# Earlier turns for a background program: VectorE runs its state-space steps in six more turns while the first input tiles are multiplied

## The chip, the core and the metric

One core of one Trainium2 chip runs the program. The metric is the device time of one execution in microseconds (us). Every time below is from the one profiled execution unless a median is named.

## The reference, cut to what matters

Two blocks run one after the other on a sequence of about 1,000 tokens of width 1024, each with a token mixer and a feed-forward part. The change lies in the first block's token mixer, in which a state-space model (S5) works on `u`, the first 512 columns of the input projection:

```python
h = rmsnorm(x, g_pre)
proj = h @ w_in
u, q, k, v, o, gi, gf, ga, gb = jnp.split(proj, IN_SPLITS, axis=-1)
y_a = jax.nn.gelu(s5_ssm(u, lam_re, lam_im, b_re, b_im, c_re, c_im, d, log_dt))
...
# in s5_ssm
ab_re = mag * jnp.cos(lam_im * dt)
ab_im = mag * jnp.sin(lam_im * dt)
...
bu_re = jnp.einsum('blgh,gph->blgp', u, bb_re)
_, _, x_re, x_im = lax.associative_scan(_complex_affine_combine, (a_re, a_im, bu_re, bu_im), axis=1)
```

The kernel does the scan over blocks of eight tokens. For that it needs, before any `u` is used, tables that depend on the weights alone: powers of the complex number `ab` for 130 block positions (`E`), its first eight powers times `bb` (the operand `Bop`), and times `c` (the operand `Cop`).

## The kernel before

**Weights and tiles.** Each weight tile (128 x 1024) goes through three steps before TensorE can use it. The SyncE queue loads it into one of two buffers `w_raw` (`load_weight`, L278), ScalarE rounds it into one of three `w_hi` (`split_act`, L287, an operation recorded at L163), and VectorE subtracts to get one of three `w_lo` (`split_dve`, L296, recorded at L166). TensorE multiplies each slice three times, w_hi by X_hi, w_hi by X_lo and w_lo by X_hi, and waits for both parts of a tile before the tile's first matmul. The load of tile i waits until both parts of tile i-2 are made; the rounding of tile i waits until TensorE is done with tile i-3, whose buffer it takes. `next_tile(L, K, ahead)` at tile i makes the part of tile i+2 (for the loads, i+4).

**The stage around the change.** After the norm of the input (`prenorm_*`), TensorE takes tiles 0 to 2 (`u0` to `u2`) together, in nine groups of matmuls: three column chunks of 264, 264 and 512 (`c` = 0, 1, 2), and in each chunk the three tiles `t` (`FIRST`, `first_pe`, L920). Then come single tiles, three chunks each: tile 3 (`u3`), tiles 4 to 7 (`v0` to `v3`), and so on (`in1_pe`, L967). `first_act` and `in1_act` move the results out on ScalarE. `first_dve` and `in1_dve` hold VectorE's share, which here is only the low parts of the weights; VectorE waits for no result of these tiles.

**The background program.** The state-space work is written as one generator for each engine (`ssm_pe`, `ssm_act`, `ssm_dve`), cut in steps by `yield`. It is laid between the instructions of the foreground when the program is built: `tick()` puts in the next `rate` steps (3 in this stage), and `pause(n)` is n steps without an instruction. On an engine the order is then fixed, and instructions run in that order; across engines only semaphores order them. In `first_dve` a tick stands ahead of each low part, and the low part of tile 3 is made after the tick of `c` = 2, `t` = 0.

When this stage begins, 9 steps of `ssm_dve` are used up (one at the start, 8 in the norm). Step 10 makes `bb` and `Bn`, step 11 the eighth power, steps 12 to 23 the table `E` (12 steps: lengths 1, 2, 4, 8 and 16 in one each, 32 in two, 64 in four, the last 2 in one), and steps 24 to 30 the seven `powers(0)` written to `ssm_W`. Then come a pause, the four steps of `outputs(0)`, another pause, and the scans.

**What hangs on it.** ScalarE has `inputs(0)` at the last tick of tile `v0` (it waits for `powers(0)` and writes `ssm_Bop`) and `outputs(0)` at the last tick of `v1` (it waits for VectorE's `outputs(0)` and writes `ssm_Cop`). VectorE's `outputs(0)` begins in the last tick of `v0` and waits for `ssm_Bop`. TensorE's first state-space matmuls (group `k`, 0, recorded at L126) stand after `v1` and wait for `ssm_Cop`. Eight dummy matmuls, and some elsewhere (`WARM`), keep TensorE running ahead of chosen groups; the groups of `u3` and of (`k`, 0) have none.

Of the kernel before, what the change touches and what calls it, by code (L numbers as in the profile page):

```python
# [303 lines left out]
def next_tile(L, K, ahead):  # L304

    i = L.tile
    L.tile += 1
    if i and ahead is not None:
        ahead(L, K, i + (4 if ahead is load_weight else 2))
    return i  # L310
# [140 lines left out]
def pause(n):  # L451
    for _ in range(n):
        yield
# [274 lines left out]
def ssm_dve(V, K):  # L728
# [60 lines left out]
    def powers(j):  # L789

        a64r, a64i = ar2[:, 64 * j:64 * j + 64], ai2[:, 64 * j:64 * j + 64]
        pw = s.pw
        V.after(d)
        if j:
            V.wait_ge(S.act, ("Cop", j - 1))
        V.vcopy(pw[:, 7, :, :], K.ssm_bb2[:, :, 64 * j:64 * j + 64]).then_inc(d)
        for tau in range(6, -1, -1):
            V.after(d)
            n = cmul(V, d, pw[:, tau, 0, :], pw[:, tau, 1, :], pw[:, tau + 1, 0, :], pw[:, tau + 1, 1, :], a64r, a64i,
                     q1[:, 0, 0:64], q1[:, 1, 0:64])  # L800
            yield
        d.at["pw", j] = n

    def outputs(j):

        w4 = lambda tau, ri: W[:, tau, ri, :].rearrange("p (k h) -> p k h", h=16)
        V.wait_ge(S.act, ("Bop", j))
        V.after(d)
        V.vcopy(w4(0, 0), bc1[:, 2, 4 * j:4 * j + 4, :]).then_inc(d)
        V.ts(w4(0, 1), bc1[:, 3, 4 * j:4 * j + 4, :], -1.0, None, MUL).then_inc(d)  # L810
        a4 = lambda a: a[:, 4 * j:4 * j + 4].unsqueeze(2).broadcast_to([128, 4, 16])
        Ar, AI = a4(ar1), a4(ai1)
        h4 = lambda a: a.rearrange("p (k h) -> p k h", h=16)
        ua, ub, uc, ud = [h4(q1[:, n // 2, 64 * (n % 2):64 * (n % 2) + 64]) for n in range(4)]
        for tau in range(8):
            V.after(d)
            V.tt(ua, w4(tau, 0), Ar, MUL).then_inc(d)
            V.tt(ub, w4(tau, 1), AI, MUL).then_inc(d)
            V.tt(uc, w4(tau, 1), Ar, MUL).then_inc(d)
            V.tt(ud, w4(tau, 0), AI, MUL).then_inc(d)  # L820
            V.after(d)
            V.tt(w4(tau + 1, 0), ua, ub, ADD).then_inc(d)
            V.tt(w4(tau + 1, 1), uc, ud, SUB).then_inc(d, ("W", j))
            if tau % 2 == 1:
                yield

    yield from powers(0)
    yield from pause(5)
    yield from outputs(0)
    yield from pause(PRE - 38)  # L830
    for j in range(4):
# [125 lines left out]
def first_dve(V, K):  # L957
    next_tile(V, K, split_dve)
    for c, t in FIRST:
        if c == 2:  # L960
            V.tick()
        V.u_done += c == 2
        if c == 2 and t < 2:
            next_tile(V, K, split_dve)
# [60 lines left out]
def in1_dve(V, K):  # L1025
    S = K.in1
    first_dve(V, K)
    for name, m in IN1[3:]:
        next_tile(V, K, split_dve)
        for c in range(3):  # L1030
            V.tick()
        if name == "u":
            V.u_done += 1
        if name in "qk":
            n = SPILL1[name, m]
            w0 = m + 4 * (name == "k")
            o, w = K.S1[n % 2][:, 0:T1], lambda j: K.vec("wqk", 4 * w0 + j)
            V.wait_ge(S.act, (name, m, 2))
            V.wait_ge(K.gpad, END)
            V.wait_ge(K.s1[n % 2], ("out", n - 2))  # L1040
            V.ts(o, K.G1[:, 3:3 + T1], w(3), K.vec("bqk", w0), MUL, ADD).then_inc(S.dve)
            for j in (2, 1, 0):
                V.after(S.dve)
                V.stt(o, K.G1[:, j:j + T1], w(j), o, MUL, ADD).then_inc(S.dve, ("conv", n))
# [2317 lines left out]
def dve_program(V, K):  # L3362
    V.bg.append(ssm_dve(V, K))
    V.step()
    V.wait_ge(K.c.cst, END)
    V.wait_ge(K.c.vec, END)
    prenorm_dve(V, K)
    V.hold, V.rate = False, RS
    in1_dve(V, K)
    V.drain()  # L3370
    gates_dve(V, K)
    V.bg.append(mgates_dve(V, K))
    V.rate = 1
    glu_dve(V, K)
    glu_over(V, K)
    V.vcopy(K.sel4[:, :, :], K.cst[0:4, 1220:1224].unsqueeze(2).broadcast_to([4, 4, 128])).then_inc(K.c.dve, "sel4")
    V.wait_ge(K.c.dve, "sel4")
    V.bg.append(mlstm_dve(V, K))
    V.rate = RM
    in2_dve(V, K)  # L3380
    V.drain()
    merge_dve(V, K)
    out1_dve(V, K)
    ffn_dve(V, K, K.F1, lambda L: None)
    in3_dve(V, K)
    heads_dve(V, K)
    out2_dve(V, K)
    ffn_dve(V, K, K.F2, lambda L: L.wait_ge(K.n4.dve, END))
    V.drain()
# [251 lines left out]
```

## Time and profile before

| | us |
|---|---|
| median of 3 runs | 3340.56 (3340.01 to 3341.56) |
| the profiled execution | 3340.01 |
| its span in the profile | 3338.2 |
| TensorE busy | 3213.3 (96%) |
| VectorE busy | 1712.5 (51%) |
| ScalarE busy | 1219.8 (37%) |
| mean granted TensorE clock | 0.994 of full speed |

PE is TensorE's matmul side, PEld its weight loads, DVE is VectorE, ACT is ScalarE, SPq is the SyncE queue. The profiled execution took 1.8 us more than its span. A matmul's recorded duration includes the pipeline's depth, so back-to-back matmuls overlap in the records and the distance from start to start is what one costs. The same holds for VectorE by a smaller overlap of some 0.08 us.

### The profile page before, as it was taken

What the parts mean: (1) busy time and instruction counts of PE and PEld (TensorE: products, weight loads), DVE (VectorE), ACT (ScalarE), POOL (GpSimd) and SP (SyncE); (2) the same over time, 40 slices, a digit from 0 to 9 for tenths busy, and PEclk for the clock granted to TensorE, in tenths of its full rate; (3) what the DMA queues carried; (4) which work ended last, traced back from release to release, by engine and by line L of the source; (5) the groups of instructions that cost most, each with busy time, mean ns of one, the idle gap of its engine ahead of it and who ended that gap; (6) DMA issues with size and microseconds to landing.
All of it is one profiled execution on the core that took longest, in us unless ns stands there. A gap on an engine that the chain in (4) does not pass through costs nothing.

```text
span 3338.2 us, 56145 instructions
## 1 busy us (share of the span) xinstructions
PE 3213.3 (96%) x24028; PEld 2673.0 (80%) x24028; DVE 1712.5 (51%) x3196; ACT 1219.8 (37%) x2166; POOL 74.6 (2%) x148
## 2 busy tenths in 40 slices
PE   8899999999999999999999999999989999999998
PEld 6788878778878888888777777777767788888886
DVE  7656253346575243435774556565635643434355
ACT  5233364442453221213452423444444431212133
POOL 0000000001000000000000000000000000000000
PEclk9999999999999999999999999999999999999999
DMA  3111121223422111112354322001003221111133
GB/s 120 71 58 65 64 96 64 77 94 115 159 95 92 54 43 53 42 53 94 122 186 152 127 77 97 26 23 36 7 14 126 95 86 54 46 56 40 56 96 113
DMA packets 85624, 262.36 MB, mean 79 GB/s; under 512 B 10592, under 2 KB 10720, under 8 KB 85248
## 3 DMA queue, kind: packets, MB, share of 16 engines
q1 hardware_dynamic: 73056, 217.78, 19.3%
q0 software_dynamic: 7424, 23.16, 2.0%
q10 hardware_dynamic: 4896, 17.84, 1.3%
q8 instruction: 190, 3.11, 0.4%
q14 instruction: 58, 0.48, 0.0%
HBM read 216.51 MB, written 42.21 MB: 78 GB/s over the span
## 4 chain that ended last, share of the span: by engine, by line
PE 79%; DVE 11%; ACT 7%; issue 2%; DMA 1%; DVEq 0%; SPq 0%; POOL 0%; ACTq 0%; POOLq 0%
PE ps L127 75%; PE ps L126 2%; DVE HB L166 2%; DVE w_lo L166 1%; PE ps L135 1%; ACT L145 1%; ACT w_hi L163 1%; DVE HB L176 1%; ACT m_D L145 1%; DVE C L176 1%; ACT a_PT L163 0%; DVE m_SS L176 0%; DVE XLA L166 0%; DMA m_D<-mq 0%; ACT L150 0%
## 5 line engine op out<-in xcount | busy, mean ns | idle before, releaser
L166 DVE TENSOR_TENSOR w_lo<-w_raw,w_hi 128x1024 fp32r<-128x1024 f32 (+3 forms) x353 | 393.7, 1115 | 369.2 <-ACT w_hi L163 367.0
L127 PE MATMUL ps<-XHA,w_hi 128*128 128x264 f32 (+3 forms) x1456 | 466.9, 321 | 9.7 <-DVE w_lo L166 5.5
L127 PE MATMUL ps<-XLA,w_hi 128*128 128x264 f32 (+3 forms) x1456 | 457.0, 314 | 0.0
L127 PE MATMUL ps<-XHA,w_lo 128*128 128x264 f32 (+3 forms) x1456 | 455.5, 313 | 0.0
L163 ACT ACTIVATE w_hi<-w_raw 128x1024 fp32r<-128x1024 f32 (+3 forms) x353 | 340.0, 963 | 309.8 <-PE ps L127 281.2
L127 PE MATMUL ps<-XHB,w_hi 128*128 128x512 f32 x920 | 368.9, 401 | 7.0 <-DVE w_lo L166 4.3
L127 PE MATMUL ps<-XHB,w_lo 128*128 128x512 f32 x920 | 359.1, 390 | 0.0
L127 PE MATMUL ps<-XLB,w_hi 128*128 128x512 f32 x920 | 359.1, 390 | 0.0
L127 PEld LDWEIGHTS ps<-XHA,w_hi 128*128 128x128 f32 x1456 | 275.4, 189 | 40.3 <-issue 15.2
L127 PEld LDWEIGHTS ps<-XLA,w_hi 128*128 128x128 f32 x1456 | 275.3, 189 | 21.1 <-issue 3.6
L127 PEld LDWEIGHTS ps<-XHA,w_lo 128*128 128x128 f32 x1456 | 275.8, 189 | 16.4
L127 PEld LDWEIGHTS ps<-XHB,w_hi 128*128 128x128 f32 x920 | 172.9, 188 | 50.4 <-issue 10.4
L127 PEld LDWEIGHTS ps<-XHB,w_lo 128*128 128x128 f32 x920 | 172.8, 188 | 36.8
L127 PEld LDWEIGHTS ps<-XLB,w_hi 128*128 128x128 f32 x920 | 173.1, 188 | 35.6 <-issue 1.9
L166 DVE TENSOR_TENSOR HB<-HB,ps 128x512 f32<-128x512 f32 (+1 forms) x136 | 88.5, 656 | 213.0 <-PE ps L127 213.0
L127 PE MATMUL ps<-X2HA,w_hi 128*128 128x512 f32 x416 | 162.6, 391 | 2.1 <-DVE w_lo L166 2.1
L127 PE MATMUL ps<-X2HB,w_hi 128*128 128x512 f32 x416 | 162.8, 391 | 0.0
L127 PE MATMUL ps<-X2HA,w_lo 128*128 128x512 f32 x416 | 162.0, 389 | 0.0
L127 PE MATMUL ps<-X2LA,w_hi 128*128 128x512 f32 x416 | 162.0, 389 | 0.0
L127 PE MATMUL ps<-X2HB,w_lo 128*128 128x512 f32 x416 | 162.0, 389 | 0.0
L127 PE MATMUL ps<-X2LB,w_hi 128*128 128x512 f32 x416 | 161.9, 389 | 0.0
L173 DVE TENSOR_SCALAR C<-G,vecs 128x512 f32<-128x512 f32 x88 | 48.0, 546 | 209.8 <-ACT G L163 209.7
(449 smaller groups left out, 5948.1 us busy)
## 6 DMA issues: line engine op xcount, KB each, us to landing
w_raw<-in_f_gate SPq DMA_DIRECT2D x66, 512.0 KB, 3.2
w_raw<-in_f_up SPq DMA_DIRECT2D x66, 512.0 KB, 3.2
w_raw<-in_w_out SPq DMA_DIRECT2D x32, 512.0 KB, 3.2
w_raw<-in_f_down SPq DMA_DIRECT2D x48, 320.0 KB, 2.9
w_raw<-in_f_down SPq DMA_DIRECT2D x32, 384.0 KB, 3.1
w_raw<-in_w_rkv SPq DMA_DIRECT2D x24, 512.0 KB, 3.3
w_raw<-in_w_attn SPq DMA_DIRECT2D x24, 512.0 KB, 3.9
w_raw<-in_w_qkvo SPq DMA_DIRECT2D x16, 512.0 KB, 3.2
```

Of the source, the lines that this page charges most:

```text
L126: return Issued(e.matmul(out, a, b, start=start, stop=stop, skip_group_check=True))
L127: return Issued(e.matmul(out, a, b, start=start, stop=stop))
L135: return Issued(self.eng and self.eng.transpose(out, src, ident))
L145: return Issued(self.eng and self.eng.activation(out, src, func, **kw))
L163: return Issued(self.eng and self.eng.activation(out, src, ACT.Copy))
L166: return Issued(self.eng and self.eng.tensor_tensor(out, a, b, op))
L173: return Issued(self.eng.tensor_scalar(out, a, s1, s2, op0, op1))
L176: return Issued(self.eng and self.eng.scalar_tensor_tensor(out=out, in0=a, scalar=s, in1=b, op0=op0, op1=op1))
```

## The change

Two lines move. `first_dve` ticks in all nine of its turns instead of in the three with `c` = 2, so 6 more ticks of 3 steps, 18 steps, are laid ahead. The pause behind `powers(0)` grows by the same 18 steps, so `outputs(0)` and all that follows keep their places among the tiles. No operation is added or taken away; only places on VectorE's list change.

```diff
     yield from powers(0)
-    yield from pause(5)
+    yield from pause(23)
     yield from outputs(0)
...
 def first_dve(V, K):
     next_tile(V, K, split_dve)
     for c, t in FIRST:
-        if c == 2:
-            V.tick()
+        V.tick()
         V.u_done += c == 2
         if c == 2 and t < 2:
             next_tile(V, K, split_dve)
```

## Rows read from the trace of the kernel before

**Rows 1.** The page: span and busy time of the engines.

```profile
span 3338.2 us, 56145 instructions
PE 3213.3 (96%) x24028; PEld 2673.0 (80%) x24028; DVE 1712.5 (51%) x3196; ACT 1219.8 (37%) x2166; POOL 74.6 (2%) x148
```

**Rows 2.** Waits, 60 to 130 us: total, times, longest.

```profile
PE ps L126 <- ACT ssm_Cop L145: 11.1, 1, 11.1
...
ACT ssm_Bop L145 <- DVE ssm_W L166: 7.2, 1, 7.2
```

**Rows 3.** VectorE's timeline: start, us, instruction, count [idle before].

```profile
59.52 0.42 DVE L166 TENSOR_TENSOR ssm_bb<-ssm_Cop,ssm_BT 128x256 f32<-128x256 f32 x1
...
68.85 1.22 DVE L166 TENSOR_TENSOR w_lo<-w_raw,w_hi 128x1024 fp32r<-128x1024 f32 x1
69.98 0.19 DVE L166 TENSOR_TENSOR HB<-HB,ssm_e 128x32 f32<-128x32 f32 x1
...
74.93 1.22 DVE L166 TENSOR_TENSOR w_lo<-w_raw,w_hi 128x1024 fp32r<-128x1024 f32 x1
76.06 0.42 DVE L166 TENSOR_TENSOR HB<-HB,ssm_e 128x256 f32<-128x256 f32 x1
...
83.71 1.22 DVE L166 TENSOR_TENSOR w_lo<-w_raw,w_hi 128x1024 fp32r<-128x1024 f32 x1
84.84 0.42 DVE L166 TENSOR_TENSOR HB<-HB,ssm_e 128x256 f32<-128x256 f32 x1
...
98.72 1.22 DVE L166 TENSOR_TENSOR w_lo<-w_raw,w_hi 128x1024 fp32r<-128x1024 f32 x1
99.86 0.22 DVE L166 TENSOR_TENSOR ssm_W<-ssm_W,ssm_a 128x64 f32<-128x64 f32 x1
...
102.27 0.36 DVE L166 TENSOR_TENSOR ssm_W<-ssm_W,ssm_q 128x64 f32<-128x64 f32 x2
104.89 0.20 DVE L186 COPY ssm_W<-ssm_bc 128x64 f32<-128x64 f32 x1 [2.26 <-ACT ssm_Bop L145]
```

**Rows 4.** TensorE's timeline: end of u2 and start of u3; after v1.

```profile
71.74 0.39 PE L127 MATMUL ps<-XHB,w_lo 128*128 128x512 f32 x1
71.97 0.28 PE L127 MATMUL ps<-XHA,w_hi 128*128 128x264 f32 x1
...
105.72 0.39 PE L127 MATMUL ps<-XHB,w_lo 128*128 128x512 f32 x1
117.18 1.93 PE L126 MATMUL ps<-ssm_Cop,ssm_Bn 128*32 128x256 f32 x16 [11.07 <-ACT ssm_Cop L145]
```

**Rows 5.** ScalarE's timeline: result of v0's last chunk, then Bop and Cop.

```profile
94.82 0.60 ACT L145 ACTIVATE m_S<-ps 128x512 f32<-128x512 f32 x1 [5.09 <-PE ps L127]
102.67 1.15 ACT L145 ACTIVATE ssm_Bop<-ssm_W,cst 128x1024 f32<-128x1024 f32 x1 [7.25 <-DVE ssm_W L166]
...
114.73 1.25 ACT L145 ACTIVATE ssm_Cop<-ssm_W,cst 128x1152 f32<-128x1152 f32 x1 [7.89 <-DVE ssm_W L166]
```

**Rows 6.** Busy time by stretch: sum, PE, PEld, DVE, ACT, POOL, PEclk, DMA share, GB/s.

```profile
34.00:59.50 25.50, 24.52 (x167) 21.96 (x166) 23.15 (x48) 13.81 (x27) 0.00 (x0) 1.00 0.16 56
...
106.10:108.70 2.60, 0.01 (x1) 0.00 (x0) 2.53 (x12) 0.74 (x2) 0.00 (x0) 1.00 0.00 0
108.70:117.10 8.40, 0.00 (x0) 0.00 (x0) 5.62 (x35) 2.37 (x3) 0.00 (x0) 0.50 0.32 126
117.10:122.20 5.10, 5.02 (x30) 3.75 (x31) 3.17 (x6) 0.97 (x2) 0.00 (x0) 0.50 0.29 103
...
131.00:340.00 209.00, 207.51 (x1864) 182.67 (x1863) 127.86 (x382) 74.81 (x109) 0.00 (x0) 1.00 0.17 65
...
925.00:930.00 5.00, 4.00 (x22) 3.65 (x23) 3.82 (x5) 2.97 (x5) 0.00 (x0) 0.79 0.02 3
930.00:935.00 5.00, 5.00 (x25) 4.11 (x24) 2.05 (x3) 2.03 (x4) 0.00 (x0) 0.87 0.30 105
```

**Rows 7.** The page: weight loads, KB each, us from issue to landing.

```profile
w_raw<-in_w_qkvo SPq DMA_DIRECT2D x16, 512.0 KB, 3.2
```

## The prediction

> **What bounds the kernel now.** The page comes first: TensorE is busy for 96% of the span [rows 1], so a change of order on VectorE (51%) counts only where TensorE waits, or would wait, for VectorE. The waits of the stretch around the change come next. From 60 to 130 us TensorE has one wait, 11.1 us for `ssm_Cop` [rows 2]. Third are the three timelines, read backwards from that wait. `ssm_Cop` starts at 114.73 on ScalarE, after VectorE's `outputs(0)`, which starts at 104.89, after `ssm_Bop`, which starts at 102.67, after the last of the seven powers, which ends at 102.27 + 0.36 = 102.63 [rows 3, 5]. From 59.52 to 102.63 VectorE has no idle time between the rows of that group: it works the background list and four low parts of weights back to back [rows 3]. So before the (k, 0) group the state-space chain sets the end, and TensorE has work beside it until about 106.1.
>
> The reader should see one more thing, on which the forecast rests: the low part of tile 3 starts at 68.85 and ends at 68.85 + 1.22 = 70.07, and TensorE comes to tile 3 at 71.97, right behind u2 [rows 3, 4]. The slack is 1.9 us.
>
> **Part one, the six extra ticks.** They look as if they belonged to the time when TensorE multiplies the first two chunks. They don't: VectorE's order is a fixed list, `first_dve` stands behind the whole norm, and the first of the background instructions starts at 59.52 [rows 3]. There is no free time ahead of it that they could fill, for VectorE is busy 23.15 of the 25.5 us from 34.0 to 59.5 [rows 6] and its instructions there stand earlier in the list. What the ticks do is move 18 steps ahead of the low part of tile 3. Before, 3 steps stood there (10 to 12); after, 7 ticks of 3, steps 10 to 30: `bb` and `Bn`, all of `E` and all of `powers(0)`.
>
> Their length is read off between the low parts:
> - steps 10 to 12: 59.52 to 68.85, 9.33 us
> - steps 13 to 15: 69.98 to 74.93, 4.95 us
> - steps 16 to 18: 76.06 to 83.71, 7.65 us
> - steps 19 to 27: 84.84 to 98.72, 13.88 us
> - steps 28 to 30: 99.86 to 102.63, 2.77 us
>
> The sum is 38.6 us [rows 3], and 0.4 either way for the joints, where a low part used to stand between two dependent instructions or a row's end overlaps the next. So the low part of tile 3 starts at 59.5 + 38.6 = 98.1 and ends at 99.3, and TensorE, ready at 71.97, stands for 99.3 - 72.0 = **27.3 us**. This is all on the path that sets the end: TensorE's own list has u3 next.
>
> Behind the late low part in VectorE's list stand those of tiles 4 and 5. That of tile 4 needs nothing new and follows at once, ending near 100.5. The load of tile 5 shares a buffer with tile 3 and moves to 99.3; it lands 3.2 us later [rows 7], and with 1.2 us each for rounding and subtracting (the length of a low part) it is whole near 105. Behind its rounding ScalarE holds the results of u3, a few us late, and TensorE has four banks to go on with. A tile of three chunks takes 11.3 us (v0's last result is out of TensorE at 94.8, v1's at 106.1 [rows 4, 5]), so tile 4 is wanted 11 us after 99.3 and tile 5 another 11 us later, and neither costs anything; were that cover gone, the price would be these 5 to 6 us.
>
> **Part two, the longer pause.** It keeps `outputs(0)` in the last tick of v0. What changes is that `powers(0)` is done long before ScalarE wants it. Before, ScalarE had v0's last chunk out at 94.82 + 0.60 = 95.42 and waited 7.25 us for it [rows 5]. After, it doesn't wait. VectorE's `outputs(0)` depends on `ssm_Bop`, `ssm_Cop` on that, and TensorE on that, each at once, so all of this comes 7.25 us sooner as seen from TensorE's tiles. What is late next is the rest of the chain: TensorE still stands 11.07 - 7.25 = 3.8 us at (k, 0) [rows 4], because `outputs(0)` can't begin before v0's last chunk. The gain is **7.25 us**.
>
> **The clock.** After the stop at 106.1 the granted clock stayed at 1.00 until 108.7, then was 0.50 for the rest of the stop and for the first 5.1 us of work, 117.1 to 122.2 [rows 6]. Those are TensorE's two levels, 2.4 and 1.2 GHz, and work for 5.1 us at half of it loses at most 2.5 us; I take 2.4. The 27.3 us stop at u3 has no dummy matmuls behind it and will be followed by the same: **+2.4 us**. The stop at (k, 0) shrinks from 11.07 to 3.8 us. The row shows the clock falling inside such a length, and at 925 to 935 us three short gaps were enough for 0.21 x 2 x 5 + 0.13 x 2 x 5 = 3.4 us at the lower level, 1.7 us lost [rows 6]. So it may lose between nothing and 2.4 us; I take 1.5, nearer those rows than nothing, and the term is 1.5 - 2.4 = **-0.9 us**.
>
> The Trainium skill, TensorE: Matmul & The Clock Gate, section "Part 1: The HAM clock gate", says that the slow clock is what TensorE has by default and that work lifts it. By that rule too the first matmuls of u3 run at 1.2 GHz, and the sum stays as it is.
>
> **Sum.** 27.3 - 7.25 + 2.4 - 0.9 = +21.55 us on the profiled execution's 3340.01, 3361.6 us. The median of the runs shown is 0.55 above that execution, which gives 3362.1, and I say **3362 us**. From (k, 0) on every engine's list is as before and its waits are for one another, not for the time of day; TensorE is busy 207.5 of the 209 us from 131 to 340 [rows 6]. So nothing there takes the delay back. The ends: the joints 0.4 each way, the clock from 1.7 - 2.4 = -0.7 to +2.4 in place of +1.5, and about 1 us for low-clock stretches later on that may fall otherwise. That gives +18 to +24, 3358.5 to 3364.5, as the likeliest case's own range.
>
> **Rivals.**
> - *Given back whole.* The wait at (k, 0) vanishes with its clock loss, because ScalarE and VectorE get through Bop, `outputs(0)` and Cop while TensorE runs v1: 27.3 + 2.4 - 11.07 - 2.4 = +16.2, 3356.8 us. For it speaks that VectorE is idle from 100.5 until then. Against it: the chain from the start of Bop to the end of Cop is 117.1 - 102.67 = 14.5 us, v1 takes 11.3.
> - *Not given back at all.* ScalarE reaches Bop late for another reason (its list also holds late results and the rounding of tiles), and (k, 0) stands as long as before: 27.3 + 2.4 = +29.7, 3370.3 us. Against it: ScalarE is idle 7.25 us there.
> - *Faster.* TensorE does not wait at u3 and the chain gains its 7.25 us, and up to 2.4 us of clock: 3333.3 to 3330.9. It decides at 11.2 us: if the steps now ahead of the low part take no longer than 71.97 - 1.22 - 59.52, TensorE never notices. They measure 38.6, so this needs most of them to run before 59.5 or behind the low part after all, that is, my count of steps to be wrong. The Trainium skill, Perfetto Trace Analysis, section "Optimization Strategy", advises finding the gap and making the work that it waits for start sooner. By that advice alone the result is this case; the rows show what the advice leaves out, another wait that the same list serves.
> - *No change.* The steps moved are mostly pauses, or the stop is some 5 to 8 us and is paid for by the 7.25: 3340.6. It needs the same miscount.
>
> **How the numbers follow.** Likeliest 0.76, given back whole 0.08, not given back 0.06, faster 0.04, no change 0.02, and 0.04 for a loss above the sum that I don't see. This kernel's measurement can tell 0.2%, 6.7 us, from no change; the slower cases are all beyond it, so slower is 0.94, same 0.02, faster 0.04. The range for 8 in 10 takes the likeliest case and the first rival, 3356 to 3366; both lie on one side.
>
> **What would show it.** Right: TensorE idle some 27 us before its first u3 matmul, released by `w_lo`; the powers ending near 98 us with no low part between 59.5 and 98; ScalarE not idle before `ssm_Bop`; a wait of about 4 us instead of 11.1 before the L126 matmuls; a granted clock of 0.50 for some us after each. Wrong: the low part of tile 3 still near 70 us (my count fails), a wait at (k, 0) near 0 or near 11 (the rivals), or new waits for `w_lo` or `w_hi` at v0 and v1 (late loads).

## The result and the profile after

| | before | after |
|---|---|---|
| median | 3340.28 us (4 runs) | 3363.62 us (4 runs, 3360.52 to 3368.23) |
| ratio, 95% interval | | 1.0072 (1.0055 to 1.0087) |
| profiled execution, span | 3338.2 us | 3361.8 us |

The change makes the kernel 23.3 us slower. The forecast was 3362, with 3356 to 3366.

The page of the changed kernel shows the same 56145 instructions [rows 1] and only 4.2 us more of TensorE's busy time, so most of the 23.6 us of span is waiting (27.7 + 3.7 - 11.1 = 20.4 us of TensorE's waits below):

```profile
span 3361.8 us, 56145 instructions
PE 3217.5 (96%) x24028; PEld 2678.6 (80%) x24028; DVE 1713.1 (51%) x3196; ACT 1219.6 (36%) x2166; POOL 74.6 (2%) x148
```

Its waits from 60 to 160 us (total, times, longest), against [rows 2]:

```profile
ACT w_hi L163 <- DMA w_raw<-in_w_qkvo: 29.8, 1, 29.8
...
PE ps L127 <- DVE w_lo L166: 27.7, 1, 27.7
...
DVE ssm_W L186 <- ACT ssm_Bop L145: 10.8, 1, 10.8
...
PE ps L126 <- ACT ssm_Cop L145: 3.7, 1, 3.7
```

TensorE has two waits here now: a new one of 27.7 us for the low part of a weight, and what is left of the 11.1 us for `ssm_Cop`. `ssm_Bop`, for which ScalarE waited 7.2 us, is gone from ScalarE's waits; VectorE, which has nothing else to do by then, waits for it instead. ScalarE's timeline, against [rows 5], shows what now sets the time of `ssm_Bop`: its place right behind v0's last chunk, without idle time between them.

```profile
124.16 0.60 ACT L145 ACTIVATE m_S<-ps 128x512 f32<-128x512 f32 x1 [5.09 <-PE ps L127]
124.65 1.14 ACT L145 ACTIVATE ssm_Bop<-ssm_W,cst 128x1024 f32<-128x1024 f32 x1
...
136.71 1.25 ACT L145 ACTIVATE ssm_Cop<-ssm_W,cst 128x1152 f32<-128x1152 f32 x1 [0.63 <-DVE ssm_W L166]
```

What is left of TensorE's wait at (k, 0) is the end of the chain that starts there. ScalarE's wait of 29.8 us is for the load of tile 5 held back by the late low part of tile 3, which shares its buffer; TensorE never waits for tile 5.

VectorE's timeline of the changed kernel, against [rows 3] (start, us, instruction):

```profile
58.87 0.42 DVE L166 TENSOR_TENSOR ssm_bb<-ssm_Cop,ssm_BT 128x256 f32<-128x256 f32 x1
...
97.55 0.35 DVE L166 TENSOR_TENSOR ssm_W<-ssm_W,ssm_q 128x64 f32<-128x64 f32 x2
97.83 2.35 DVE L166 TENSOR_TENSOR w_lo<-w_raw,w_hi 128x1024 fp32r<-128x1024 f32 x2
103.53 1.23 DVE L166 TENSOR_TENSOR w_lo<-w_raw,w_hi 128x1024 fp32r<-128x1024 f32 x1 [3.36 <-ACT w_hi L163]
114.84 1.23 DVE L166 TENSOR_TENSOR w_lo<-w_raw,w_hi 128x1024 fp32r<-128x1024 f32 x1 [10.08 <-ACT w_hi L163]
126.86 0.20 DVE L186 COPY ssm_W<-ssm_bc 128x64 f32<-128x64 f32 x1 [10.80 <-ACT ssm_Bop L145]
```

No low part stands between 58.87 and 97.83. The background steps 10 to 30 take 97.83 - 58.87 = 38.96 us in one piece, and then the low parts of tiles 3 and 4 come together (x2). TensorE's timeline, against [rows 4]:

```profile
71.08 0.39 PE L127 MATMUL ps<-XHB,w_lo 128*128 128x512 f32 x1
99.19 0.56 PE L127 MATMUL ps<-XHA,w_hi 128*128 128x264 f32 x1 [27.72 <-DVE w_lo L166]
99.54 0.42 PE L127 MATMUL ps<-XLA,w_hi 128*128 128x264 f32 x1
...
103.28 0.42 PE L127 MATMUL ps<-XHA,w_hi 128*128 128x264 f32 x1
103.50 0.39 PE L127 MATMUL ps<-XLA,w_hi 128*128 128x264 f32 x1
103.72 0.30 PE L127 MATMUL ps<-XHA,w_lo 128*128 128x264 f32 x1
103.86 0.29 PE L127 MATMUL ps<-XHA,w_hi 128*128 128x264 f32 x1
...
135.06 0.39 PE L127 MATMUL ps<-XHB,w_lo 128*128 128x512 f32 x1
139.16 1.94 PE L126 MATMUL ps<-ssm_Cop,ssm_Bn 128*32 128x256 f32 x16 [3.72 <-ACT ssm_Cop L145]
```

The 264-column matmuls start 0.22 us apart until 103.7 and 0.12 us apart from then on. Busy time by stretch gives the granted clock for it (sum, PE, PEld, DVE, ACT, POOL, PEclk, DMA share, GB/s), against [rows 6]:

```profile
71.90:74.60 2.70, 0.00 (x0) 0.00 (x0) 2.63 (x14) 0.71 (x1) 0.00 (x0) 1.00 0.00 0
74.60:99.40 24.80, 0.21 (x1) 0.24 (x2) 24.19 (x108) 0.00 (x0) 0.00 (x0) 0.54 0.00 0
99.40:104.00 4.60, 4.60 (x23) 4.60 (x24) 1.24 (x2) 1.06 (x1) 0.00 (x0) 0.53 0.72 224
...
135.90:139.00 3.10, 0.00 (x0) 0.00 (x0) 0.74 (x5) 2.47 (x3) 0.00 (x0) 0.82 0.42 172
139.00:142.00 3.00, 2.84 (x20) 1.57 (x21) 1.88 (x3) 1.06 (x2) 0.00 (x0) 0.50 0.00 0
142.00:144.00 2.00, 2.00 (x11) 2.00 (x10) 1.29 (x4) 0.00 (x0) 0.00 (x0) 0.50 0.80 260
```

The clock is at the lower level for the first 4.5 us of u3, and again from within the stop of 3.7 us at (k, 0) until past 144.

### The profile page after: what moved, and what is told of

Read it like the earlier page. It is cut to its first block, busy times and chain, and to the rows that moved or that the text cites. A ratio compares the mean times of both kernels' runs of the same rounds, so it can differ in the third digit from the quotient of the medians.

```text
span 3361.8 us, 56145 instructions
## 1 busy us (share of the span) xinstructions
PE 3217.5 (96%) x24028; PEld 2678.6 (80%) x24028; DVE 1713.1 (51%) x3196; ACT 1219.6 (36%) x2166; POOL 74.6 (2%) x148
## 4 chain that ended last, share of the span: by engine, by line
PE 79%; DVE 11%; ACT 7%; issue 2%; DMA 1%; DVEq 0%; SPq 0%; POOL 0%; ACTq 0%; POOLq 0%
PE ps L127 76%; PE ps L126 2%; DVE HB L166 2%; DVE w_lo L166 1%; PE ps L135 1%; ACT w_hi L163 1%; ACT L145 1%; DVE HB L176 1%; ACT m_D L145 1%; DVE C L176 1%; ACT a_PT L163 0%; DVE m_SS L176 0%; DVE XLA L166 0%; DMA m_D<-mq 0%; ACT L150 0%
## 5 line engine op out<-in xcount | busy, mean ns | idle before, releaser
L127 PEld LDWEIGHTS ps<-XHA,w_hi 128*128 128x128 f32 x1456 | 276.3, 190 | 68.4 <-issue 43.3
```

The lines of the kernel that those rows point to most:

```text
L127: return Issued(e.matmul(out, a, b, start=start, stop=stop))
```

## The experiments

The expectations below call the prediction's account the list theory: VectorE runs a fixed list, and the next low part in it waits for all that stands ahead of it. Times of whole executions spread by 6 to 11 us within one kernel, so each profile is also read at one mark: the start of TensorE's (k, 0) group, and that of its first matmul with `ssm_Bop` (the BU group), both counted from VectorE's first background instruction (`ssm_bb`, 59.52 us before, 58.87 after). Later than that, from BU to the end, the kernels take 3212.5 to 3218.5 us in no order that follows from their edits. The kernel before was run again beside each group of kernels; its median there stands in brackets.

| kernel | (k, 0) | against before | BU | against before | median us (before beside it) | ratio, 95% interval |
|---|---|---|---|---|---|---|
| before | 57.66 | | 64.10 | | | |
| changed kernel | 80.29 | +22.63 | 86.91 | +22.81 | 3363.62 (3340.28) | 1.0072 (1.0055 to 1.0087) |
| one_tick | 56.67 | -0.99 | 63.33 | -0.77 | 3336.60 (3339.82) | 0.9989 (0.9980 to 0.9998) |
| two_ticks | 64.02 | +6.36 | 70.93 | +6.83 | 3348.51 (3339.82) | 1.0024 (1.0012 to 1.0036) |
| low3_first | 69.57 | +11.91 | 76.42 | +12.32 | 3353.57 (3338.54) | 1.0042 (1.0026 to 1.0057) |
| after_busy | 79.82 | +22.16 | 86.72 | +22.62 | 3359.53 (3339.82) | 1.0065 (1.0051 to 1.0079) |
| after_busy64 | 78.28 | +20.62 | 83.91 | +19.81 | 3357.04 (3340.68) | 1.0054 (1.0041 to 1.0066) |
| powers_first | 55.61 | -2.05 | 61.78 | -2.32 | 3339.71 (3339.82) | 0.9999 (0.9990 to 1.0008) |
| early_all | 46.51 | -11.15 | 59.44 | -4.66 | 3335.61 (3338.54) | 0.9998 (0.9989 to 1.0006) |
| early_split | 46.51 | -11.15 | 51.68 | -12.42 | 3326.49 (3340.68) | 0.9955 (0.9941 to 0.9968) |

**One extra tick (one_tick).** The kernel before with one of the six ticks:

```diff
-    yield from pause(5)
+    yield from pause(8)
...
-        if c == 2:
+        if c == 2 or (c, t) == (1, 2):
             V.tick()
```

> The kernel before with one of the six extra ticks (3 steps, 4.95 us of VectorE) and 3 more steps of pause. List theory: TensorE stops at u3 for 4.95 - 1.9 = 3.0 us (a clock drop of up to 1.5 us with it), and all of it is given back at (k, 0), because the powers still end near 101.5 to 102.6 us and the chain Bop, outputs(0), Cop still sets the end there: the wait of 11.1 us shrinks to about 7 to 8. One low part fewer stands ahead of the powers, 1.1 us sooner. Net -1 to +0.5 us, no change. Rival, a stop at u3 is lost whole: +3 us or more at u3 and still 11 us at (k, 0).

Its two waits on TensorE's timeline:

```profile
74.51 0.36 PE L127 MATMUL ps<-XHA,w_hi 128*128 128x264 f32 x1 [3.15 <-DVE w_lo L166]
...
115.42 1.93 PE L126 MATMUL ps<-ssm_Cop,ssm_Bn 128*32 128x256 f32 x16 [6.70 <-ACT ssm_Cop L145]
```

A stop of 3.15 us at u3 (3.0 expected), and at (k, 0) 6.70 us in place of 11.07: the mark lies 0.99 us earlier than before, as the list theory has it. That a stop is lost whole is refuted for short ones: TensorE only waits in another place. The median is 3.2 us lower, the mark 1.0; the interval reaches from 0.7 to 6.7 us. The stop of 3.15 us lies between 71.4 and 74.5, and no clock is lost in it or behind it:

```profile
70.00:75.00 5.00, 1.85 (x10) 1.30 (x10) 4.89 (x26) 1.11 (x1) 0.00 (x0) 1.00 0.00 0
75.00:80.00 5.00, 5.00 (x43) 5.00 (x43) 4.90 (x20) 1.63 (x2) 0.00 (x0) 1.00 0.34 108
```

**Two extra ticks (two_ticks).** As above with `(c, t) in ((1, 1), (1, 2))` and `pause(11)`.

> The kernel before with two of the six extra ticks (4.95 + 7.65 = 12.6 us of VectorE ahead of the low part of tile 3). List theory: TensorE stops 12.6 - 1.9 = 10.7 us at u3, with 2.4 us of clock behind it; ScalarE no longer waits for the powers, so 7.25 us come back and 3.8 us stay at (k, 0). Net +10.7 + 2.4 - 7.25 = +5.9 us, 3346, up to 0.9 less if the clock does not fall at (k, 0). Rival, the stop is lost whole: +13 us. Rival, all is given back up to 11 us: +2 us.

The stops are 10.92 us (10.7 expected) and 3.72 (3.8), the mark +6.36 (+5.9). Both rivals, +13 and +2, fail. The median is up 8.7 us with an interval of 4 to 12. The same 3.72 us is left at (k, 0) in the changed kernel and in low3_first, behind stops of 27.7 and 17.4 us. So one tick shows the giving back, and the larger doses where it ends: at 7.4 us, which is 11.07 - 3.72.

**The low part of tile 3 on time (low3_first).** The changed kernel with that one instruction ahead of the 18 steps, which now stand ahead of tile 4's:

```diff
-    for c, t in FIRST:
+    for n, (c, t) in enumerate(FIRST):
         V.tick()
         V.u_done += c == 2
-        if c == 2 and t < 2:
+        if n == 0:
+            next_tile(V, K, split_dve)
+        if c == 2 and t == 1:
             next_tile(V, K, split_dve)
```

> The changed kernel with the low part of tile 3 back behind the first 3 steps; the other 18 steps now stand ahead of the low part of tile 4. List theory (what costs is the next low part in VectorE's list, whichever it is): no stop at u3, a stop at v0 until 59.5 + 38.6 + 2 x 1.2 = 100.5 us, where TensorE arrives at 83.3: 17.2 us, 2.4 us of clock, then the same 3.8 us at (k, 0). Net +17.2 + 2.4 - 7.25 = +12.4 us, 3352.7. Rival, tile 3 alone is what hurt (its buffer also holds back the load of tile 5): with it on time the kernel is back at 3333 to 3340.

```profile
100.27 0.56 PE L127 MATMUL ps<-XHA,w_hi 128*128 128x264 f32 x1 [17.41 <-DVE w_lo L166]
```

No stop at u3, 17.41 us at v0 (17.2 expected), the mark +11.9 (+12.4). Nothing is special about tile 3 or the buffer it shares; the next low part in the list pays for the block of steps, less the 11.3 us of one more tile that TensorE can work meanwhile.

**TensorE kept busy through the stop (after_busy, after_busy64).** The changed kernel with dummy matmuls ahead of the wait at u3:

```diff
 WARM = {
+    ("u", 3, 0): 60,
```

> The changed kernel with 60 dummy matmuls ahead of TensorE's wait for tile 3, so that it is at work for about 26 of the 27.7 us. If the clock loss of 2.4 us at u3 is real and comes from the stop: granted clock 1.00 when u3 begins, its first 264-column chunk at 0.12 us from start to start from the first matmul on, and the (k, 0) group 2.2 to 2.4 us sooner than in the changed kernel, 3361 against 3363.6. Rival, the clock costs nothing here: same distance from the start of u3 to (k, 0) as in the changed kernel. If the dummies run past 99 us, u3 starts later by what they overrun.

The 60 dummies ended at 97.4 and left 1.8 us without work. The clock was 1.00 when u3 began at 99.24, fell all the same at about 100.5, and came back just before 104:

```profile
99.00:100.00 1.00, 0.76 (x6) 0.80 (x7) 1.00 (x2) 0.00 (x0) 0.00 (x0) 1.00 0.00 0
100.00:101.00 1.00, 1.00 (x9) 1.00 (x8) 0.23 (x1) 0.00 (x0) 0.00 (x0) 0.75 0.88 254
101.00:102.00 1.00, 1.00 (x6) 1.00 (x6) 0.00 (x0) 0.00 (x0) 0.00 (x0) 0.50 0.86 324
```

Only 0.5 us was saved up to (k, 0), so neither side was decided. The repeat had 64:

> The changed kernel with 64 dummy matmuls ahead of the wait at u3, so that at most 0.3 us of the 27.7 us stays without work (with 60 dummies a gap of 1.8 us was left, and the clock still fell 1.3 us after the start of u3, for 3.3 us). If the clock loss at u3 comes from the stop: granted clock 1.00 from 71 to 110 us, and from the start of u3 to (k, 0) 2.1 us less than the 39.97 us of the changed kernel. Rival, the clock falls there whatever TensorE does: again some 3 us at 0.50 within u3.

```profile
71.00:99.00 28.00, 28.00 (x131) 24.62 (x130) 27.25 (x130) 1.13 (x1) 0.00 (x0) 1.00 0.00 1
99.00:105.00 6.00, 5.90 (x46) 5.50 (x46) 2.70 (x3) 1.62 (x2) 0.00 (x0) 1.00 0.56 178
105.00:110.00 5.00, 5.00 (x26) 4.26 (x26) 0.26 (x1) 0.66 (x1) 0.00 (x0) 1.00 0.32 105
135.20:138.00 2.80, 0.30 (x8) 0.21 (x12) 0.01 (x1) 2.75 (x3) 0.00 (x0) 1.00 0.46 190
138.00:142.00 4.00, 4.00 (x30) 3.33 (x23) 3.17 (x6) 0.59 (x1) 0.00 (x0) 0.57 0.23 85
```

Now the clock stays at 1.00 through u3. From the start of u3 (99.75) to (k, 0) (137.70) it is 37.95 us against 139.16 - 99.19 = 39.97, so the clock's share of the loss at u3 is 2.0 us. The dummies did not delay u3: it starts 40.33 us behind VectorE's first background instruction, 40.32 us in the changed kernel. The stop at (k, 0) was as long as in the changed kernel (3.71 us), but the clock was still 1.00 when it ended and fell only after 138. From (k, 0) to BU it took 5.63 us where the changed kernel took 6.62, so a stop of the same length cost 1.0 us less here, and BU comes 3.0 us earlier than in the changed kernel.

**The powers first (powers_first).** Part two without part one, or so I thought (part two of the change is a longer pause and moves nothing by itself): no extra tick, `powers(0)` ahead of the table `E`. In the kernel before, `E`'s temporary lies in the memory of `Bop`, so it moves too.

```diff
-    cur, e8, r8, q2 = (c1, n1), K.ssm_e8, K.ssm_r8, s.q2
+    cur, e8, r8, q2 = (c1, n1), K.ssm_e8, K.ssm_r8, K.ssm_q1
...
     yield from powers(0)
+    yield from table()
     yield from pause(5)
```

(`table()` is the loop that fills `E`, unchanged.)

> The kernel before (no extra tick) with powers(0) laid ahead of the table E, whose temporary moves to another buffer (in the kernel before it lies in Bop's memory). This is part two of the change without part one. List theory: no stop at u3; ScalarE does not wait for the powers; the wait at (k, 0) falls from 11.1 to 3.8 us: -7.25 us, 3333, with the same or up to 2.4 us less of clock loss there. Rival, the gain at (k, 0) exists only because TensorE arrives later: wait still 11 us, 3340.

The forecast fails: the wait at (k, 0) is 9.02 us, not 3.8, and the mark moves by 2.05 us, not 7.25. VectorE's timeline shows why:

```profile
66.67 0.23 DVE L186 COPY ssm_W<-ssm_bb 128x128 f32<-128x128 f32 x1
...
95.11 1.22 DVE L166 TENSOR_TENSOR w_lo<-w_raw,w_hi 128x1024 fp32r<-128x1024 f32 x1
102.02 0.20 DVE L186 COPY ssm_W<-ssm_bc 128x64 f32<-128x64 f32 x1
```

The powers begin at 66.67 and `ssm_Bop` is no longer late. But `outputs(0)` (the copy at 102.02) stands behind all of `E`, and it starts without idle time ahead of it, at 43.3 us from the first instruction where it was 45.4. The wait for `Bop` had been covering a list that is full anyway. Where TensorE comes late, that list runs out: in the changed kernel VectorE is idle for 10.80 us ahead of the same copy.

**Powers and outputs first (early_all).** `powers(0)`, five steps of `E`, `outputs(0)`, the rest of `E`; `E`'s temporary moved as in powers_first; on ScalarE `Bop` and `Cop` earlier.

```diff
     yield from powers(0)
-    yield from pause(5)
+    rest = table()
+    for _ in range(5):
+        next(rest)
+        yield
     yield from outputs(0)
+    yield from rest
+    yield from pause(5)
...
# ssm_act
-    yield from pause(33)
+    yield from pause(16)
     inputs(0)
-    yield from pause(8)
+    yield from pause(18)
     outputs(0)
+    yield from pause(7)
```

> The kernel before without extra ticks, with VectorE's list in the order powers(0), five steps of E, outputs(0), the rest of E, E's temporary in another buffer, and ScalarE's Bop moved from the last tick of v0 to the first of u3 and its Cop to the first tick of v1. List theory: both parts of the wait at (k, 0) go, 11.1 us and its 2.4 us of clock, and u3 is on time: 3340.3 - 13.5 = 3326.8. Rival, the moved work makes a low part or a result late elsewhere (a wait of several us at v0, v1 or v2): 3330 to 3340.

The rival was right that a wait would turn up elsewhere, though not at v0, v1 or v2. The wait at (k, 0) is gone (mark -11.15), and 6.5 us of it come back as a wait of 8.75 us ahead of the BU matmuls, for `ssm_Dop`:

```profile
114.20 2.35 DVE L166 TENSOR_TENSOR w_lo<-w_raw,w_hi 128x1024 fp32r<-128x1024 f32 x2
116.47 1.76 DVE L186 COPY ssm_Dop<-ps 32x256 f32<-32x256 f32 x4
```

The rest of `E` runs until 114.2, two low parts follow, and the copy that frees TensorE's bank stands behind them.

**The rest of E behind the copy (early_split).** The last five steps of `E` move behind that copy, where VectorE had 16.9 us without work before.

```diff
-    yield from rest
-    yield from pause(5)
+    for _ in range(2):
+        next(rest)
+        yield
+    yield from pause(10)
...
-        yield from pause(4)
-        yield from pause(2)
+        if not j:
+            yield from rest
+            V.after(d)
+        yield from pause(6 if j else 1)
```

> The previous kernel (powers(0), five steps of E, outputs(0) early) with the last five steps of E, 9.2 us of VectorE, moved from ahead of the first copy to ssm_Dop to behind it, into the 17 us in which VectorE waits for the BU results in the kernel before. If VectorE's list as a whole is what sets the end of this stretch: no wait at (k, 0), and the wait for ssm_Dop of 8.7 us falls to about 1.3 us, so TensorE's first BU matmul starts some 11 to 12.5 us sooner than in the kernel before as counted from VectorE's first background step, 3327 to 3329 us. Rival, the wait of 8.7 us has another cause (the low parts ahead of the copy, or a bank): it stays, 3336.

```profile
105.84 1.07 PE L126 MATMUL ps<-ssm_Cop,ssm_Bn 128*32 128x256 f32 x16
...
111.01 1.18 PE L127 MATMUL ps<-HB,ssm_Bop 32*128 32x130 f32 x32 [0.98 <-DVE ssm_Dop L186]
```

One wait of 0.98 us is left, no clock loss (16 matmuls in 1.07 us in place of 1.93 [rows 4]), the BU mark 12.42 us earlier (11 to 12.5 expected). So the steps of `E` caused the wait of 8.75 us. The median is 3326.49 (3327 to 3329 expected) against 3340.68, 14.2 us less, ratio 0.9955 (0.9941 to 0.9968). It beats both kernels.

## Why the prediction was right

Measured against each term (the marks, from the profiles):

| term | forecast | measured |
|---|---|---|
| stop at u3 | +27.3 | +27.72 |
| given back at (k, 0) | -7.25 | 11.07 - 3.72 = -7.35 |
| clock at u3 | +2.4 | +2.1, and 2.0 by after_busy64 |
| clock at (k, 0) | -0.9 | +0.2 |
| sum up to BU | +21.55 | +22.8 |

- **The ticks do not fill the time of the first two chunks.** Right: the first background instruction still comes right behind the norm, and the low part of tile 3 ends 38.96 + 1.2 us behind it. The clock term at u3 comes from u3 to the end of v1: 135.45 - 99.19 = 36.26 us against 106.1 - 71.97 = 34.13 before.
- **Loads and results late, without cost.** Right: tile 5's low part ends at 104.8 and TensorE has no wait at v0 or v1.
- **What is given back.** The size was right. The limit was right too: `outputs(0)` can't begin before v0's last chunk, and 3.72 us were left behind each of the three stops of 10.9, 17.4 and 27.7 us. one_tick and two_ticks show the rule behind it in this kernel: about the first 7.4 us of a stop cost nothing. But the reason was told too simply. I put the gain down to the longer pause, with the powers done before ScalarE wants them. powers_first shows that powers done in time are by themselves worth 2.05 us, since VectorE's list ahead of `outputs(0)` is as long in either order. The other 5.3 us came back only because TensorE arrived so late that the list had run out. The number came out because the stop was far longer than 7.4 us; read off the same wait in a kernel without a stop, it was wrong (7.25 forecast, 2.05 measured).
- **Clock.** Right at u3. At (k, 0) the term was mis-sized: I expected the shorter stop to cost 0.9 us less, and it cost 0.2 more. From (k, 0) to BU it takes 6.62 us after and 6.44 before. The stop of 3.72 us still reached the lower level and the work after it began there. In after_busy64, behind the same stop, the work began at 1.00 and lost 1.0 us less, so the term was not fixed by the stop's length.
- **The rest of the program** adds 1.4 us in the profiled pair (from BU on 3216.0 against 3214.6), within the spread of all kernels there; ahead of the marks, VectorE's first background instruction came 0.65 us earlier. Together that is 22.81 + 1.44 - 0.65 = 23.6 us of span. The 3363.6 of the median against 3362 lies within what those stretches do from run to run.

No rival came about: there was 3.7 us left at (k, 0), neither 0 nor 11.

## What to carry to other kernels

- Work laid into a fixed instruction list "while another engine is busy" runs when the list gets there, not when the other engine is at that place. Before moving steps, add up all that then stands ahead of the next instruction that someone waits for, and hold it against the slack (here 38.6 us against 11.2).
- A wait further down the path pays for a new stop, but only up to the point where something else sets the end. Two or three small doses find that point.
- If a list is full, changing its order gains only where steps that nobody wants yet move behind one that is wanted: here the last steps of a table moved behind the short copy that TensorE wanted at once, into 17 us in which VectorE had nothing to do.

## What was not expected of the hardware

- After a gap of 1.8 us behind 26 us of steady matmuls the granted clock went to 0.50 for about 3.4 us, from 100.5 on, when TensorE had already been at work again for 1.3 us (after_busy). With no gap it stayed at 1.00 (after_busy64). But the longer stop of 3.15 us at u3 in one_tick cost nothing: the clock stayed at 1.00, and from the start of u3 to the end of v1 it took 34.2 us, as before (34.1). The stops of 3.7 us at (k, 0) cost 1.0 us less in after_busy64 than in the changed kernel. So the length of a stop alone did not decide what it costs; what did is not shown by these runs.
- From BU to the end the ten profiled kernels take 3212.5 to 3218.5 us for the same instructions (in early_split with five steps of `E` more). The stretches at the lower clock lie at other places in each: in the kernel before, 665 to 670 and around 2475 us, in the changed one among others 445 to 450 and 1655 to 1660 us. Added up from 150 us on, the time at the lower level is about 16 us in powers_first, which has the shortest rest (3212.5 us), 25 in the kernel before (3214.6), 34 in the changed one (3216.0) and 37 in after_busy, which has the longest (3218.5). So the two go together, if not in strict order over all ten; that the one makes the other was not tested.
